# Block products in the down projection of a two-fold feed-forward: three chunks instead of two, and a new split of the helper work

## The reference, cut to what matters

```python
def swiglu(x, wg, wu, wd):
    return (jax.nn.silu(x @ wg) * (x @ wu)) @ wd

x = x + 0.5 * swiglu(rms_norm(x, g_ffn1), w_ffn1_gate, w_ffn1_up, w_ffn1_down)   # inner width 2816
x = x + mixer(rms_norm(x, g_mix))
x = x + 0.5 * swiglu(rms_norm(x, g_ffn2), w_ffn2_gate, w_ffn2_up, w_ffn2_down)
y = rms_norm(x, g_final)
```

## Time and profile before

| what | value |
|---|---|
| median of 3 runs | 1065.37 us (1064.82 to 1065.58) |
| the profiled execution, first to last instruction | 1063.2 us |
| PE busy | 1055.5 us, 99% |
| DVE busy | 684.2 us, 64% |
| ACT busy | 465.7 us, 44% |
| POOL busy | 189.8 us, 18% |
| DMA | 127.84 MB, mean 120 GB/s |
| chain that ended last | PE 98% |

### The profile page before, as it was taken

The page is one execution under the profiler, slowest core; times in us unless marked ns, Lnnn a source line. Parts: engine busy times, 40 slices in busy tenths (PEclk is TensorE's granted clock), DMA queues, the critical chain, the costliest instruction groups (busy, mean ns, idle before and its releaser), DMA issues.

```text
span 1063.2 us, 20510 instructions
## 1 busy us (share of the span) xinstructions
PE 1055.5 (99%) x8425; PEld 1052.1 (99%) x8425; DVE 684.2 (64%) x1170; ACT 465.7 (44%) x822; POOL 189.8 (18%) x169
## 2 busy tenths in 40 slices
PE   9999999999999999999999999999999999999997
PEld 8999999999999999999999999999999999999997
DVE  6997752367866676655655556598875236777555
ACT  6466641256652345433222224446664114666323
POOL 1122100112201211210332222212210002220111
PEclk9999999999999999999999999999999999999999
DMA  8589482479833377445454224547958328892422
GB/s 225 121 172 200 100 196 84 96 159 177 176 82 96 64 135 139 71 68 80 69 80 75 67 78 62 140 91 170 206 110 187 92 82 166 178 180 52 124 75 84
DMA packets 245493, 127.84 MB, mean 120 GB/s; under 512 B 9228, under 2 KB 243892, under 8 KB 245272
## 3 DMA queue, kind: packets, MB, share of 16 engines
q1 hardware_dynamic: 207032, 106.79, 41.6%
q0 software_dynamic: 38288, 19.72, 14.6%
q10 hardware_dynamic: 80, 0.02, 0.0%
HBM read 123.22 MB, written 3.29 MB: 119 GB/s over the span
## 4 chain that ended last, share of the span: by engine, by line
PE 98%; DMA 1%; DVE 0%; SPq 0%; issue 0%; ACT 0%
PE dense L623 52%; PE dense L768 31%; PE core_banks L768 5%; PE core_banks L623 3%; PE dense L691 1%; PE core_banks L928 1%; PE core_banks L943 1%; PE dense L824 1%; PE core_banks L946 1%; PE core_banks L918 1%; DMA x_tok<-in_x_prompt 1%; PE core_banks L955 0%; PE core_banks L912 0%; PE core_banks L914 0%; PE core_banks L805 0%; PE core_banks L666 0%
## 5 line engine op out<-in xcount | busy, mean ns | idle before, releaser
L1481 DVE TENSOR_TENSOR w_lo<-w_raw,w_hi 128x1024 fp32r<-128x1024 f32 (+2 forms) x118 | 131.7, 1133 | 55.1 <-ACT w_hi L1068 55.0
L1068 ACT ACTIVATE w_hi<-w_raw 128x1024 fp32r<-128x1024 f32 (+2 forms) x118 | 105.2, 904 | 89.3 <-PE dense L623 81.4
L623 PE MATMUL dense<-h_hi,w_hi 128*128 128x272 f32 x684 | 142.5, 290 | 0.0
L623 PE MATMUL dense<-xg_hi,w_hi 128*128 128x272 f32 x672 | 142.2, 293 | 0.0
L623 PE MATMUL dense<-h_lo,w_hi 128*128 128x272 f32 x684 | 141.1, 287 | 0.0
L623 PE MATMUL dense<-h_hi,w_lo 128*128 128x272 f32 x684 | 140.9, 287 | 0.0
L623 PE MATMUL dense<-xg_lo,w_hi 128*128 128x272 f32 x672 | 138.9, 288 | 0.0
L623 PE MATMUL dense<-xg_hi,w_lo 128*128 128x272 f32 x672 | 138.8, 287 | 0.0
L768 PE MATMUL dense<-x_op_hi,w_lo 128*128 128x272 f32 x432 | 124.6, 289 | 0.0
L768 PE MATMUL dense<-x_op_hi,w_hi 128*128 128x272 f32 x432 | 124.5, 288 | 0.0
L768 PE MATMUL dense<-x_late_hi,w_lo 128*128 128x272 f32 x432 | 124.5, 288 | 0.0
(11 more groups left out here) (341 smaller groups left out, 2212.1 us busy)
## 6 DMA issues: line engine op xcount, KB each, us to landing
w_raw<-in_w_ffn_up SPq DMA_DIRECT2D x91, 256.0 KB, 3.6
w_src<-in_w_ffn_gate SPq DMA_DIRECT2D x90, 256.0 KB, 4.6
w_raw<-in_w_in SPq DMA_DIRECT2D x32, 512.0 KB, 8.9
w_raw<-in_w_ffn_down SPq DMA_DIRECT2D x32, 384.0 KB, 4.0
w_raw<-in_w_ffn_down SPq DMA_DIRECT2D x32, 320.0 KB, 3.5
w_src<-in_w_ffn_gate POOLq DMA_DIRECT2D x36, 256.0 KB, 5.2
w_raw<-in_w_ffn_up POOLq DMA_DIRECT2D x36, 256.0 KB, 5.8
w_raw<-in_w_out SPq DMA_DIRECT2D x8, 512.0 KB, 3.9
```

What stands on the lines that cost most here:

```text
L623: last = nc.tensor.matmul(out[:, half, 0:TH], w[:, s % 4, k, :], x(kt)[:, half * TH:(half + 1) * TH], start=start and n == 0 and m == 0, s ...
L1068: nc.scalar.activation(w_hi[:, s % 4, 0:k_tiles(s), :], raw, ACT.Copy).then_inc(w_hi_ready, 1)
L1481: nc.vector.tensor_tensor(w_lo[:, s % 4, 0:nk, :], w_raw[:, s % RAW, 0:nk, :], w_hi[:, s % 4, 0:nk, :].bitcast(F32), ALU.subtract).then_in ...
```

## The change

The 22 inner tiles go in three chunks of 8, 8 and 6: plain units and pairs 0 to 3, pairs 4 to 11, pairs 12 to 17. The down products of the first two chunks become block products too: 4 steps per chunk (`down_pair`), each making two output tiles from 8 inner tiles in 7 products of 12 matmuls, with the same buffers, banks, loads and helper order as a pair (a step has a running number g). DVE adds each product from its bank onto xT (`take_down`). The weight blocks of down come the same way: five loads, two accumulating DMAs, two DVE sums. The third chunk's down products stay ordinary, 6 k-tiles per output tile.

The block form needs seven operands of h per group of two inner tiles (h_op, 272 columns each): three are h itself, four are sums. POOL makes the sums (`sum_h`), ACT the high parts (`h_to_hi`), DVE the low parts (`h_to_lo`); for the two groups of plain tiles POOL makes the low parts of the sums (`sums_to_lo`). POOL also makes two of the sums of x (`make_late_sums`) that DVE made before.

In a pair, product 4 is no longer copied. `gate_second` and `up_second` read it from the bank, and PE waits for them ahead of product 6. The other copies go straight to where the result is made, and the buffer `kept` is gone. The square of x for the mixer's norm moves from DVE to ACT in the first feed-forward's tail, except for the last tile. The diff, cut:

```diff
-    PAIRS = (range(0, 8), range(8, 18))
-    FC, F0 = (12, FT - 12), (0, 12)
-    DOWN_K = [[(0, 6), (6, 12)], [(0, 5), (5, FT - 12)]]
-    UNITS_F, TILES_F = 2 * STD + 4 * DT, 2 * STD + 2 * DT
+    PAIRS = (range(0, 4), range(4, 12), range(12, 18))
+    FC, F0 = (8, 8, FT - 16), (0, 8, 16)
+    TAIL_TILES = FC[2]
+    UNITS_F, TILES_F = 2 * STD + DT, 2 * STD + DT
...
-    NEGATED = (2, 6)
-    KEPT = (0, 1, 2, 4)
+    COPIED = (0, 1, 2)
...
+    FIRST_ORDER = (0, 1, 3, 2, 4, 5, 6)
...
+    H_OPS = (3, 6, 0, 1, 2, 5, 4)
+    H_SUMS = (1, 2, 5, 4)
+    H_COPIES = (3, 6, 0)
...
+        def down_quarter(w, c, d):
+            return lambda k, m: w_rows(w)[:, F0[c] + k:F0[c] + FC[c]:2, (2 * d + m) * P:(2 * d + m + 1) * P]
...
                     if o == 4:
-                        pe.wait_ge(product_copied, 4 * P_ + 3)
+                        pe.wait_ge(product_copied, 3 * P_ + 3)
                     if o == 6:
-                        pe.wait_ge(product_copied, 4 * P_ + 4)
+                        if e == 0:
+                            pe.wait_ge(pair_gate_made, 3 * Q + 2)
+                        else:
+                            pe.wait_ge(pair_up_taken, 3 * Q + 2)
...
+            def down_pair(n, c, d):
+                g, D = step_of_down(n, c, d), down_index(n, c, d)
+                e = g % 2
+                last_k = KH - 1
+                def part(o, ks):
+                    return block_products(n, g, o, ks, lambda k: h_op[:, k, 0, o, :], lambda k: h_op[:, k, 1, o, :])
+                if d >= 2:
+                    pe.wait_ge(down_taken, BLOCKS * (D - 1))
+                elif d == 1:
+                    pe.wait_ge(pair_h_made, 2 * (pair_index(n, PAIRS[c][-1]) // 2 + 1))
+                else:
+                    pe.wait_ge(pair_gate_silu, 3 * (pair_index(n, PAIRS[c][-1]) // 2 + 1))
+                    before = c * GROUPS + last_k - 1
+                    pe.wait_ge(h_op_lo_dve, dve_los(n, before))
+                    pe.wait_ge(h_op_lo_pool, pool_los(n, before))
+                    for o in OPENS:
+                        pe.wait_ge(block_lo, BLOCKS * g + o + 1)
+                        part(o, range(last_k))
+                    for o in OPENS:
+                        h_ready(n, before + 1, o)
+                        part(o, range(last_k, KH)).then_inc(product_done, 1)
+                    pe.wait_ge(down_taken, BLOCKS * D + 1)
+                    pe.wait_ge(block_lo, BLOCKS * g + 3)
+                    h_ready(n, before + 1, 2)
+                    part(2, range(KH)).then_inc(product_done, 1)
+                    pe.wait_ge(down_taken, BLOCKS * D + 2)
+                    pe.wait_ge(block_lo, BLOCKS * g + 6)
+                    part(5, range(KH // 2))
+                    pe.wait_ge(down_taken, BLOCKS * D + 4)
+                    h_ready(n, before + 1, 4)
+                    part(4, range(KH)).then_inc(product_done, 1)
+                    h_ready(n, before + 1, 5)
+                    part(5, range(KH // 2, KH)).then_inc(product_done, 1)
+                    pe.wait_ge(down_taken, BLOCKS * D + 5)
+                    pe.wait_ge(block_lo, BLOCKS * g + BLOCKS)
+                    h_ready(n, before + 1, 6)
+                    part(6, range(KH)).then_inc(product_done, 1)
+                    return
+                for o in range(BLOCKS):
+                    if o in (2, 4, 6):
+                        pe.wait_ge(down_taken, BLOCKS * D + o - 1)
+                    pe.wait_ge(block_lo, BLOCKS * g + o + 1)
+                    part(o, range(KH)).then_inc(product_done, 1)
...
                 for o in range(BLOCKS):
-                    if o in KEPT:
+                    if o in COPIED:
                         copy_product(n, p, o)
-                    next_hi(n, c, p, o)
-                    if e == 0 and p - 2 in PAIRS[c]:
+                    next_hi(n, g, o)
+                    if follows and c < 2:
+                        if o == 1:
+                            h_to_hi(n, k, 3)
+                            h_to_hi(n, k, 6)
+                        if o == 2:
+                            h_to_hi(n, k, 0)
+                            h_to_hi(n, k, 1)
                         if o == 3:
-                            pair_h_to_hi(c, p - 2, Q - 1, 1)
+                            h_to_hi(n, k, 2)
+                            h_to_hi(n, k, 5)
+                        if o == 4:
+                            h_to_hi(n, k, 4)
...
             def gate_second(n, p):
-                dve.wait_ge(product_copied, 4 * pair_index(n, p) + 4)
-                nc.vector.tensor_tensor(pair_gate[1][:, TH:T], kept[:, 0, 3, :], kept[:, 0, 1, :], ALU.add).then_inc(pair_gate_made, 1)
+                dve.wait_ge(product_done, done_by(step_of_pair(n, p), 4))
+                dve.wait_ge(product_copied, 3 * pair_index(n, p) + 2)
+                out = pair_gate[1][:, TH:T]
+                nc.vector.tensor_tensor(out, pair_banks(0)[0], out, ALU.subtract).then_inc(pair_gate_made, 1)
...
             def up_second(n, p):
-                dve.wait_ge(product_copied, 4 * pair_index(n, p) + 4)
-                nc.vector.tensor_tensor(pair_h[1][:, TH:T], kept[:, 1, 3, :], kept[:, 1, 1, :], ALU.add)
+                dve.wait_ge(product_done, done_by(step_of_pair(n, p), 4))
+                dve.wait_ge(product_copied, 3 * pair_index(n, p) + 2)
+                out = pair_h[1][:, TH:T]
+                nc.vector.tensor_tensor(out, pair_banks(1)[0], out, ALU.subtract).then_inc(pair_up_taken, 1)
...
+            def take_down(n, c, d, o):
+                g, D = step_of_down(n, c, d), down_index(n, c, d)
+                rank = order_of(g).index
+                m, half = ((0, 0), (1, 1), (1, 0), (0, 0), (1, 1), (1, 0), (0, 1))[o]
+                factor = (0.5, -0.5, -0.5, 0.5, 0.5, 0.5, -0.5)[o]
+                dve.wait_ge(product_done, done_by(g, o))
+                if o in (3, 4, 5):
+                    dve.wait_ge(down_taken, BLOCKS * D + rank((0, 1, 2)[o - 3]) + 1)
+                x = xT[:, 2 * d + m, half * TH:(half + 1) * TH]
+                nc.vector.scalar_tensor_tensor(x, pair_banks(g % 2)[BANK[o]], factor, x, ALU.mult, ALU.add).then_inc(down_taken, 1)
...
                 x_to_lo(n, 6)
-                plain_h_to_lo(n, STD - 1)
-                block_to_lo(n, 1, 0)
-                block_to_lo(n, 1, 1)
+                block_to_lo(n, g + 1, 0)
+                block_to_lo(n, g + 1, 1)
                 gate_first(n, 0, Q)
-                block_to_lo(n, 1, 2)
-                sum_t4(n, 1)
-                block_to_lo(n, 1, 3)
+                for o in H_COPIES:
+                    h_to_lo(n, 1, o)
+                block_to_lo(n, g + 1, 2)
+                sum_t4(g + 1)
                 gate_second(n, 0)
-                block_to_lo(n, 1, 4)
-                block_to_lo(n, 1, 5)
+                block_to_lo(n, g + 1, 3)
+                block_to_lo(n, g + 1, 4)
+                block_to_lo(n, g + 1, 5)
                 gate_third(n, 0)
-                block_to_lo(n, 1, 6)
+                block_to_lo(n, g + 1, 6)
...
+                    if follows and c < 2 and o == 2:
+                        for h_o in H_COPIES:
+                            h_to_lo(n, group_of(p) - 1, h_o)
+                    if follows and c < 2 and o in (4, 5, 6):
+                        for h_o in {4: (1,), 5: (2, 5), 6: (4,)}[o]:
+                            h_to_lo(n, group_of(p) - 1, h_o)
+                    if follows and c == 2 and o in (4, 6):
+                        tail_to_lo(n, p // 2 - 1, 1 if o == 4 else 0)
+                    next_lo(n, g, o)
...
+            def down_pair(n, c, d):
+                g, k = step_of_down(n, c, d), c * GROUPS + GROUPS - 1
+                if d == 0:
+                    up_last(n, PAIRS[c][-1], pair_index(n, PAIRS[c][-1]) // 2)
+                    sum_t2(g + 1)
+                    for o in (3, 6, 0, 1, 2):
+                        h_to_lo(n, k, o)
+                    take_down(n, c, d, 0)
+                    h_to_lo(n, k, 5)
+                    h_to_lo(n, k, 4)
+                    take_down(n, c, d, 1)
+                    take_down(n, c, d, 3)
+                    next_lo(n, g, 0)
+                    next_lo(n, g, 1)
+                    take_down(n, c, d, 2)
+                    next_lo(n, g, 2)
+                    sum_t4(g + 1)
+                    next_lo(n, g, 3)
+                    take_down(n, c, d, 4)
+                    next_lo(n, g, 4)
+                    take_down(n, c, d, 5)
+                    next_lo(n, g, 5)
+                    take_down(n, c, d, 6)
+                    next_lo(n, g, 6)
+                    return
+                for o in range(BLOCKS):
+                    take_down(n, c, d, o)
+                    if o == 0:
+                        sum_t2(g + 1)
+                    if o == 3:
+                        sum_t4(g + 1)
+                    next_lo(n, g, o)
...
+            def make_late_sums(n):
+                pool.wait_ge(x_made, 10 * n + 8)
```

(24 more changed lines are left out.)

## The result

Over four runs each, the changed kernel takes 1139.63 us in the median (1139.28 to 1142.11), the kernel before on the same chip 1065.28: a ratio of 1.070, 95% interval 1.0685 to 1.0715. It is slower, as forecast, but by 74 us instead of 50, and outside the range.

The account below looks back on a forecast made before the run. PE's instruction stream, busy 99%, was taken as the bound. 1063.2 - 24.1 (fewer matmuls) + 71.8 (waits) + 1.7 (end) = 1112.6 us profiled; with the median 2.2 above the span, 1115 us, range 1084 to 1130.

Parts of the forecast that it names:

- the chain at bank 0: Product 6 waits until DVE has read product 4 from the bank: 2.19 us of fixed lengths in 1.31 of room.
- What bounds the kernel, and the saving: PE's instruction stream is the time; 192 fewer matmuls in the kernel at 0.1255 us each save 24.1 us.
- Bank 0 in up steps: PE loses 0.88 us at product 6 in eight up steps of each feed-forward, 7.0 us.
- Gate steps: Loss each: 0.52 us without h group, 0.74 in chunk 3; with h group 2.8, of which 1.1 order, 1.7 contention.
- The first pair and the plain stage: First pair of each feed-forward: 3.8 us from DVE's order plus 2.2 contention, 6.0; plain stage nothing (bound 0 to 3).
- The part from contention: In the first pair, eight POOL operations shutting out DVE cost between 0 and 5.4 us; 2.2 taken.
- The first block down step: First step of each block down product, two per feed-forward: 2.3 us without contention, 2.2 more with it, 4.5 each.
- Block down steps 2 to 4: Each taking is done a product ahead, so nothing is lost; 10.54 us each.
- The end: Behind the last block products, DVE's scaling of part 0 and tile 6's transposes lose 1.7 us (1.2 and 0.5).
- A, light contention: Rival: POOL slips into DVE's gaps, only the queue order costs; 1088 us, chance 0.18.
- B, faster: Rival: bank 0 handoff costs nothing, as ACT and DVE reach block 4 sooner than the rows say; 1042, chance 0.08.
- C: Rival, starved sums: accumulating DMAs land after the DVE sums needing them, 24 us more; 1139, chance 0.10.

Follow-up runs that it names:

- before_bank_read: The kernel before, with product 4 no longer copied by ScalarE but read from its bank by gate_second and up_second, PE's product 6 waiting for that: 1101.28 us.
- second_early: The changed kernel with gate_second and up_second moved right behind gate_first or up_first in VectorE's queue in pairs: 1103.43 us, ratio 1.036.
- sums_write_only: The changed kernel with all GpSimd sums and low parts in the feed-forwards replaced by memsets of the same tiles, sums left out: 1093.83 us, ratio 1.026.

## Why the prediction was right or wrong

The direction and the chain at bank 0 were right. Two steps failed. The sum let a wait cost PE its own length and nothing more; the matmuls behind the waits ran slower, by 20.8 us. And it let DVE enter the first pair on time, with the plain stage priced at nothing; the first pairs waited 11.4 us each instead of 6.0.

**What bounds the kernel, and the saving: right.** PE's stream was the time, and the stage between the feed-forwards' block steps, with 192 matmuls less, is shorter by 24.1 us, which is 0.1255 us for each.

**Bank 0 in up steps: right in mechanism and size.** 0.88 forecast, 0.87 measured, in 16 steps each time. before_bank_read has the same wait, second_early hasn't.

**Gate steps: right.** 0.52 forecast and 0.52 measured without an h group; 0.74 against 0.65 (once 0.80) in chunk 3. With an h group, 2.84 against 2.42. The uncontended part, 1.1, came out as 1.04 in sums_write_only.

**The first pair and the plain stage: the second step that failed.** I forecast 6.0 us each. The waits were 11.4 and slower matmuls added 2.1. The part from the order, 3.8, is the 3.8 at product 6 of sums_write_only. The part from contention I put at 2.2 by choice, between 0 and 5.4. It was 7.3 (11.4 less the 4.1 of waits in sums_write_only), beyond my upper bound, for three reasons. DVE came in 5.1 and 2.8 us late from the plain stage, where I had counted nothing, because its low parts are made a unit ahead. In the pair, POOL's low parts of one h group and the sums and low parts of the next ran beside it: three x operands took 0.6 more each and two low parts 1.1 together. And the late DVE result held up ACT, so PE waited at product 2, a path that I hadn't looked at. How the 7.3 divide among these, no run shows.

**The first block down step: size about right.** 4.5 forecast, 3.6 of wait and 1.5 of slower matmuls measured (each step, four of them). Of the uncontended 2.3, sums_write_only shows 1.8. Block down steps 2 to 4 lose 0.03 us each, as forecast.

**The clock: the term that was missing, and the larger of the two errors.** The waits sum to 75.6 us, against 71.8 forecast, with errors that cancel (first pairs 10.8 too low, gate steps and block down steps 6.7 too high). The 20.8 us of slower matmuls had no place in the sum at all. A wait costs PE some 0.09 us more than its length even at full clock (up steps of chunk 3: 10.53 + 0.87 + 0.09), for the 45 waits of over 0.3 us some 4 us; the other 17 or so are half clock. I read 1.00 in the earlier trace rows and carried it over, though these rows were of a PE that never waited. For the profiled execution the forecast was 1112.6. With 3.8 for the waits, 20.8 for the slower matmuls, 1.3 for the small gaps in the steps, 0.7 for the plain stage and 1.2 at the end it becomes 1140.4, against a span of 1140.3; the median of the four runs lies 2.5 us below this execution's time.

**The end:** 1.7 forecast, 2.9 measured, half of it seen directly: the last tile waits 1.9 us for its squares, where it waited 0.5.

**The range.** Its upper edge takes 2.3 us more for each first pair, where the bound of 5.4 in place of the 2.2 chosen is 3.2 more. That alone would not have reached 1139.6: the waits of the first pairs went beyond the bound, and nothing in the range stood for the clock.

**The rivals.** A, light contention, at 1088, comes near the kernel without POOL's reads (1093.8), which has 8.2 us of slower matmuls in it; in the changed kernel POOL didn't slip into DVE's gaps. B, faster, failed for the reason given against it: the chain behind product 4 doesn't fit. C gave 1139, the measured time, but is wrong all the same: no wait of DVE for a DMA appears in its list, and the block down steps 2 to 4, which would have suffered too, are clean. A time that fits says nothing for a mechanism.

**What stays open.** Why a wait of 2.4 us was followed by a stretch at half clock in 5 of the 8 gate steps with an h group and not in the others. No experiment set waits between 1.5 and 3.5 us one at a time. PE's 0.7 us in the plain stage and 1.5 of the 2.9 at the end were not followed up.

## What to carry to other kernels

When a bank is released by another engine than before, write down that engine's queue from the event that makes the data ready to the instruction that releases: what stands in between is paid by TensorE in every step, and moving one instruction forward gets it back. When TensorE begins to wait for several microseconds at a time, add a term for the clock behind each wait; a granted clock read from a stretch without waits doesn't carry over. And work taken from VectorE onto GpSimd, at a place where VectorE is full, can cost VectorE more than it takes away: here VectorE was busy for less time with all of the sums in its own queue than with GpSimd making them. Look for this also in the stage ahead: VectorE can fall behind there without TensorE losing anything yet.

## What was not expected of the hardware

- A wait of TensorE of 3.5 to 3.8 us cost 1.5 to 2.5 us of slower matmuls behind it, one of 5.3 to 5.8 only 1.5 to 1.6: part of the half-clock stretch lay in the longer wait itself. The shorter wait was not the cheaper one in this respect.
- GpSimd's sums of 272 columns took 0.98 to 1.16 us in the median by their lines, where half of the 1.36 for 544 columns had let me expect 0.68. The shortest took 0.84. Beside them, VectorE's 272-column subtraction went from 0.44 to 0.97 in the mean.
- GpSimd's writes of the same 272 columns, 0.33 us each in the median, left VectorE's subtraction at its 0.44.
